# Block one's attention: three buffers for turned probabilities, two places for diagonals of denominators

## What is computed

```python
def attend(qblk):        # one of two blocks of 128 queries, 8 query heads, 2 key heads
    s = jnp.einsum('bqkgd,bskd->bkgqs', qblk, k, preferred_element_type=jnp.float32) * scale
    p = jax.nn.softmax(s, axis=-1).astype(v.dtype)
    return jnp.einsum('bkgqs,bskd->bqkgd', p, v)
```

## Time and profile before

| | us |
|---|---|
| Median of 3 runs | 2303.95 |
| Lowest and highest run | 2303.86, 2306.98 |
| The profiled execution's own time | 2306.2 |
| Its span in the profile | 2304.9 |
| TensorE busy in it | 1940.7 (84%) |
| VectorE busy | 987.1 (43%) |
| ScalarE busy | 670.5 (29%) |
| DMA queue of the loads, share of 16 engines | 70.4% |

### The profile page before, as it was taken

The page is one execution under the profiler, slowest core; times in us unless marked ns, Lnnn a source line. Parts: engine busy times, 40 slices in busy tenths (PEclk is TensorE's granted clock), DMA queues, the critical chain, the costliest instruction groups (busy, mean ns, idle before and its releaser), DMA issues.

```text
span 2304.9 us, 29024 instructions
## 1 busy us (share of the span) xinstructions
PE 1940.7 (84%) x12348; PEld 1349.2 (59%) x12348; DVE 987.1 (43%) x1237; ACT 670.5 (29%) x817; POOL 66.9 (3%) x144
## 2 busy tenths in 40 slices
PE   7899998555666655666689999999999999999998
PEld 4767872111111111111137999779998999788997
DVE  4754651000000000000005657876657656876656
ACT  4432430000000000000004444564445444455444
POOL 0000000000000000000001001010001000100000
PEclk9999999888777777777799999999999999999999
DMA  9255899999999999999997564335554554425552
GB/s 372 71 182 212 333 374 423 434 429 432 431 431 431 432 429 433 431 430 432 430 401 270 197 210 146 129 137 183 194 182 164 190 195 173 154 87 179 194 193 88
DMA packets 53489, 647.44 MB, mean 281 GB/s; under 512 B 5936, under 2 KB 6448, under 8 KB 10096
## 3 DMA queue, kind: packets, MB, share of 16 engines
q1 hardware_dynamic: 53360, 645.59, 70.4%
HBM read 644.52 MB, written 1.05 MB: 280 GB/s over the span
## 4 chain that ended last, share of the span: by engine, by line
PE 58%; DMA 31%; DVE 6%; ACT 2%; issue 1%; POOL 0%; SPq 0%; DVEq 0%; ACTq 0%; POOLq 0%
DMA wide_b<-in_experts 29%; PE PS L489 14%; PE PS L491 13%; PE PS L490 13%; PE PS L953 4%; PE PS L988 4%; DMA ring<-in_wgt 1%; DVE low L1896 1%; DMA ring<-in_fg 1%; PE PS L931 1%; PE PS L507 1%; PE PS L642 1%; PE PS L486 1%; DMA ring<-in_wmod 1%; PE PS L855 1%
## 5 line engine op out<-in xcount | busy, mean ns | idle before, releaser
L1896 DVE TENSOR_TENSOR low<-ring,WH 128x2048 fp32r<-128x2048 f32 (+1 forms) x163 | 372.0, 2282 | 182.6 <-ACT WH L2285 180.1
L489 PE MATMUL PS<-XH,WH 128*128 128x256 f32 x1408 | 396.5, 282 | 3.2 <-DVE XL L1928 3.1
L490 PE MATMUL PS<-XL,WH 128*128 128x256 f32 x1408 | 395.0, 281 | 0.0
L491 PE MATMUL PS<-XH,low 128*128 128x256 f32 x1408 | 393.0, 279 | 0.0
L2285 ACT ACTIVATE WH<-ring 128x2048 fp32r<-128x2048 f32 (+1 forms) x164 | 313.2, 1910 | 31.2 <-PE PS L988 18.7
L489 PEld LDWEIGHTS PS<-XH,WH 128*128 128x128 f32 x1408 | 264.5, 188 | 6.7 <-issue 5.0
L491 PEld LDWEIGHTS PS<-XH,low 128*128 128x128 f32 x1408 | 267.2, 190 | 0.0
L490 PEld LDWEIGHTS PS<-XL,WH 128*128 128x128 f32 x1408 | 264.3, 188 | 1.4
L1878 DVE TENSOR_TENSOR T1S<-T1S,PS 128x512 f32<-128x512 f32 x16 | 11.0, 687 | 547.2 <-PE PS L953 547.2
L953 PE MATMUL PS<-ring,big 128*32 128x512 f32 x936 | 137.1, 736 | 52.4 <-DMA ring<-in_experts 52.4
L2560 ACT ACTIVATE T1S<-PS 128x512 f32<-128x512 f32 x16 | 9.6, 597 | 540.2 <-PE PS L953 540.2
(11 more groups left out here) (447 smaller groups left out, 2747.7 us busy)
## 6 DMA issues: line engine op xcount, KB each, us to landing
wide_b<-in_experts SPq DMA_DIRECT2D x30, 4096.0 KB, 23.7
wide_a<-in_experts SPq DMA_DIRECT2D x29, 4096.0 KB, 23.7
ring<-in_experts SPq DMA_DIRECT2D x28, 4096.0 KB, 24.0
ring<-in_fg SPq DMA_DIRECT2D x44, 1024.0 KB, 5.0
ring<-in_fu SPq DMA_DIRECT2D x44, 1024.0 KB, 5.0
ring<-in_fd SPq DMA_DIRECT2D x44, 1024.0 KB, 5.0
ring<-in_wmod SPq DMA_DIRECT2D x22, 1024.0 KB, 5.8
ring<-in_wgt SPq DMA_DIRECT2D x12, 1024.0 KB, 8.5
```

Source lines behind the costliest of these rows:

```text
L489: t.matmul(o, l[0], r[0], start=start, stop=False, skip_group_check=True)
L490: t.matmul(o, l[0], r[1], start=False, stop=False, skip_group_check=True)
L491: return t.matmul(o, l[1], r[0], start=False, stop=stop, skip_group_check=True)
L1896: own(v.tensor_tensor(low[:, w.slot.index, 0:size], w.flat, WH[:, w.slot.index, 0:size].bitcast(f32), ALU.subtract).then_inc(*c.wl.up()), ...
```

## The change

The turned probabilities get a third buffer, and the buffers go round by heads: head h is in buffer h modulo 3, whichever engine copies it. The third buffer is the second half of `AT`. For that the diagonals of denominators, which had four places in the two halves of `AT`, keep two, in its first half, and the wait before a diagonal is written is gone. VectorE's copy at odd g waits for `c.pv` of g-3; ScalarE's wait is as before.

```diff
-        scale = AT[:, :, :].rearrange("p m (a i c) -> p (m a) i c", a=2, i=2)
+        scale = AT[:, 0, :].rearrange("p (a i c) -> p a i c", a=2, i=2)
+        pts = [PT[:, 0, :], PT[:, 1, :], AT[:, 1, :]]
...
-                            x = t.matmul(PS[64 * i:64 * i + 64, 9 - b, 128:256], cd[:, 2, 0:64], scale[:, n % 4, i, :],
+                            x = t.matmul(PS[64 * i:64 * i + 64, 9 - b, 128:256], cd[:, 2, 0:64], scale[:, n % 2, i, :],
...
-                                             PT[:, i, k * 128:k * 128 + 128], start=k == 0, stop=k == 3,
+                                             pts[(g - 3 + i) % 3][:, k * 128:k * 128 + 128], start=k == 0, stop=k == 3,
...
                         V.wait_ge(c.ptp, g)
-                        if g > 2:
-                            V.wait_ge(c.pv, g - 2)
-                        own(v.tensor_copy(PT[:, 0, :], PS[:, 2, :]).then_inc(*c.pcv.up()), c.pcv)
+                        if g > 3:
+                            V.wait_ge(c.pv, g - 3)
+                        own(v.tensor_copy(pts[(g - 1) % 3], PS[:, 2, :]).then_inc(*c.pcv.up()), c.pcv)
...
                         own(v.reciprocal(r, r))
-                        if n > 3:
-                            V.wait_ge(c.pv, 2 * (n - 3))
-                        own(v.tensor_tensor(scale[:, n % 4], ident.unsqueeze(1).to_broadcast([128, 2, 128]),
+                        own(v.tensor_tensor(scale[:, n % 2], ident.unsqueeze(1).to_broadcast([128, 2, 128]),
...
-                                            scale[:, n % 4, 0, :], ALU.mult).then_inc(*c.attv.up()), c.attv)
+                                            scale[:, n % 2, 0, :], ALU.mult).then_inc(*c.attv.up()), c.attv)
...
-                        own(copy(PT[:, 1, :], PS[:, 3, :]).then_inc(*c.pca.up()), c.pca)
+                        own(copy(pts[(g - 1) % 3], PS[:, 3, :]).then_inc(*c.pca.up()), c.pca)
...
-                        own(copy(scale[:, n % 4, 0, :], PS[:, 5 - n % 2, 128:256]).then_inc(*c.atta.up()), c.atta)
+                        own(copy(scale[:, n % 2, 0, :], PS[:, 5 - n % 2, 128:256]).then_inc(*c.atta.up()), c.atta)
```

## The result

| | before | changed |
|---|---|---|
| Median of the runs shown first | 2303.95 (3 runs) | |
| Median of the runs of the comparison | 2301.40 (20 runs, 2299.04 to 2306.98) | 2298.65 (20 runs, 2292.18 to 2303.53) |
| Profiled execution, own time | 2306.2 | 2299.03 |
| Its span | 2304.9 | 2297.7 |

The ratio of the changed kernel to before is 0.9984, 95% interval [0.9976, 0.9991]: 0.16% faster, some 3.7 us of 2301, with an interval from 2.1 to 5.5 us. The difference of the medians is 2.75 us. The forecast was 2300.8 us, 0.14% under its base, in a range of 2298.0 to 2304.0, with 0.80 for a change within 0.2%. The median lies in the range, and the 0.16% lies within 0.2%, but the interval leaves no room for "no difference", which the prediction called the likeliest verdict.

A forecast was written before the change was run, and what follows sets the result against it. TensorE, then DMA, then TensorE bound the kernel; in the first stretch the chain ran through VectorE's copy. Terms 1.07 + 0.82 + 1.28 = 3.17 us, from 2303.95, gave 2300.8 us, range 2298.0 to 2304.0.

The forecast's parts named there:

- the last copy: VectorE's copy at 186.71 us: no wait there, late weights ahead of it, so nothing gained.
- Place one: VectorE's copy at 107.46 us: without its 1.97 us wait, TensorE's next filter product starts 1.07 us earlier.
- Place three: VectorE's copy at 134.95 us: TensorE, idle 1.62 us for the gate eviction behind it, gains 0.82 us.
- Place five: VectorE's copy at 160.54 us: waited 1.31 us, moves to 159.26, and TensorE gains 1.28 us.
- Places two, four and six: Copies at 121.70, 148.58 and 174.18 us: waits of 3.43 and together 5.0 us, whose removal gains nothing.
- The clock: TensorE's half-clock stretch from 189 to 196 us, costing about 3.0 us, stays because the 2.2 us idle before it stays.
- rival (b): The half-clock stretch goes, saving a further 3.0 us: 2297.8 us; chance 0.14.
- Rival (a): Gate-weight loads behind each place take back the gain: 2302.1 us, or 2304.0 if all goes; chance 0.22.
- The sign of being wrong that the prediction named: A landing takes the copy's place in the chain of waits, or 3 us at 185 us are gone behind the experts.
- Rival (c): Half clock falls on TensorE-bound work: one more stretch gives 2303.8 us, from the second on slower, 2306.8; chance 0.05.
- held by its transposes instead: The copy waits for the transposes of L751, so the change does not do what it says; counted within chance 0.22.
- Through the DMA-bound stretch: Sixth to twenty-first slice, paced by the experts' weights: an earlier start ends it as much earlier, 3 us.

The follow-up runs named there:

- place one alone: Changed kernel with the old wait back for every g over 3, so gone only at g = 3: 2301.10 us, ratio 0.9995 to before.
- 9 products: Kernel before with 9 unit-matrix products added on TensorE behind the values of g = 15: 2302.78 us, ratio 1.0001 to before.
- the first experiment: Changed kernel with VectorE's even-head copy again waiting for its own step's values, three buffers kept: 2302.53 us, ratio 1.0003 to before.
- the reverse experiment: Changed kernel with the old wait kept at g = 3, 7, 11, 15 and gone at 5, 9, 13: 2301.48 us, ratio 1.0003 to before.
- 18 products: Kernel before with 18 unit-matrix products added on TensorE behind the values of g = 15: 2301.79 us, ratio 1.0002 to before.

## Why the prediction was right or wrong

**Where it failed.** Two steps failed, and the first made the forecast wrong: the step from the sum to "the likeliest verdict is no difference". The second is a term of the sum, the last copy, which was put at nothing and is taken up below.

The first step rests on "0.2%, or 4.6 us, is about what a measurement of this kernel can tell from no change". With 20 runs the interval was 0.075% to either side, 1.7 us. A gain of 3.17 us, which I held to be the likeliest, lies outside of it, and so does the measured one of some 3.7 us (0.16%), although both are within 0.2%. From three runs of before, spread over 3.1 us, the resolution of a larger comparison can't be read; I used the spread as if it were the error. The forecast of the sum was one of a gain, and the chances did not say so.

**The base.** 2303.95 was the median of three; 20 runs have 2301.40, and all 111 of before in this document 2301.9. The forecast of 2300.8 is 2.15 too high: 2.55 of it is the base, less 0.4, since the medians differ by 2.75 and the sum had 3.17. The range held the median with 0.65 to spare.

**Place one**, 1.07 us: right. 1.09 alone in the trace. The link that limits it is the one named, ScalarE's copy of the third hyena tile, as VectorE's view of the changed kernel has it:

```profile
108.17 0.69 DVE L1651 COPY ATG<-PS 128x512 f32<-128x512 f32 x1
109.73 0.42 DVE L1452 TENSOR_SCALAR XN<-XN,base 128x256 f32<-128x256 f32 x1 [0.87 <-ACT XN L2284]
```

**Place three**, 0.82: right, and steady. The gate product stands 43.71 or 43.72 behind the first scores in all three profiles of such kernels, against 45.62.

**Place five**, 1.28: the mechanism is right, and that the size was met is luck. It is 1.29 in the profile, but the term hangs on a landing, which the prediction took from one execution. In before and in the first profile of the changed kernel the weights were first read 8.33 and 8.32 us after their issue. In the other two profiles of such kernels it was 7.95, which gave 0.37 more than in the first, and 9.41, which took 1.1. With the wait put back it was 9.33, and there the copy stood only 0.31 us until the values, not 1.31.

**Places two, four and six**, nothing: right, 1.0003 with these alone, and all gate products in place.

**The last copy**, "Nothing is gained": the term that was mis-sized. I read it off one execution, in which the gate weights were late (issued at 172.85, 10.10 us) and hid the copy. Where the weights came in time, the copy was held there as in the other places: it stood 0.54 us until the values with the wait put back, 0.59 with place one alone and 0.48 with 9 products, with first reads at 9.08, 9.03 and 9.14 us. TensorE's wait behind it was 1.61 and 1.62 in the first two. With the change it was 0.88, 1.20 and 0.89. The last gate product was 96.77 behind the first scores with the wait and 92.84 without, 3.93 apart and not 3.17. The 0.76 between are the copy's 0.54 and 0.24 from a load that came earlier (8.84 against 9.08). The 4.54 between the two first profiles has before's late landing in it besides.

**The clock.** "By the rows the 2.2 stay, the slow stretch with them" was wrong for the profiled execution, rival (b) happened in it, and as an account of the mean neither is shown. Over all profiles the last gate wait and what followed are: 2.21, 2.29 and 2.71 us with a stretch under full clock behind (0.51, 0.53 and 0.76 over 7 us), 1.61, 1.62, 1.20, 0.89 and 0.88 without, and none when the wait was filled. The Trainium skill ("TensorE: Matmul & The Clock Gate", section on the HAM clock gate) has the point where the clock changes at the start of a kernel differ from run to run of one kernel. Here the profiles with the wait differ among themselves too, in the middle of the program; but so do their waits, with the landing, and the cause stays open. How much of the mean it makes stays open as well, with 1.6 us as the most that filling the wait can have given.

**Rival (a)**, loads that take the gain back, was wrong as the main story and right in single executions. The sign of being wrong that the prediction named did come, a landing ahead of the copy in the chain at place five (147.98 us), and in that profile it took nothing of the 3.17; in a later one it took 1.1. **Rival (c)** did not come about. That the copy might be held by its transposes instead holds for one copy and 0.18 us, besides the first copy, which always was.

**Through the DMA-bound stretch**: right. A lead of 4.65 us at its start was 4.30 at its end. Ahead of it a lead is less safe: see the 3.93 and 1.98 us of the first experiment.

## What to carry to other kernels

A long wait on an engine is worth what stands behind it in that engine's program and is waited for elsewhere: 8.4 us of waits were worth nothing that can be told, 4.1 us and the last copy were worth some three, and moving one eviction out from behind the waiting copy was worth no less (0.9981) than a third buffer that lets the copy go (0.9984). Cost a place at nothing only if what hides it is there in every execution: a transfer that lands late in one profile hides a wait that others pay. The same holds for a place that is given its full price beside a load that landed early. And when a gain of a tenth of a per cent is forecast, take the chance of seeing it from the error of a mean over the runs of the comparison, not from the spread of three.

## What was unexpected of the hardware

The time from the issue of the same 1 MB of gate weights, behind two others of 1 MB, to the first read of it varied between executions of nearly the same kernel: at the last place ScalarE began 8.84 us after the issue in the changed kernel, 9.08 with the wait put back, 10.18 in before and 10.26 in the reverse experiment. At place five it was 7.95 to 9.41 in three profiles of kernels whose programs differ in three waits at most. At the last place this moves TensorE's wait from 1.6 to 2.3 us, and it is as large as the terms of the sum. A product of the unit matrix in full precision, 128 columns, shows as two matmul instructions: 18 products gave this row, twice what I had sized.

```profile
185.35 4.29 PE L486 MATMUL PS<-base 128*128 128x128 f32 x36
```

Single landings scatter, but the DMA-bound stretch is steady: 779.4 to 780.0 us in eleven profiles, within 0.1%.
